# Modulation products of a two-block transformer kernel: column chunks side by side in the free dimension, against four chunks stacked in the partitions

## The reference, cut to what matters

```python
mod = silu(c) @ w_mod_2 + b_mod_2       # (2048) @ (2048, 6 * 2048)
h * (1 + scale) + shift                 # modulate()
```

## Time and profile before

| | |
|---|---|
| median of 3 runs | 2852.14 us |
| the profiled execution: its own time | 2854.0 us |
| its span, first to last instruction | 2852.2 us |
| granted TensorE clock, mean | 0.994 of 2.4 GHz |
| TensorE busy | 2803.9 us, 98% |
| VectorE busy | 2003.3 us, 70% |
| ScalarE busy | 1381.3 us, 48% |
| DMA, mean | 217 GB/s, share of 16 engines in the SP and ScalarE queues 65.7% and 1.5% |

### The profile page before, as it was taken

The page is one execution under the profiler, slowest core; times in us unless marked ns, Lnnn a source line. Parts: engine busy times, 40 slices in busy tenths (PEclk is TensorE's granted clock), DMA queues, the critical chain, the costliest instruction groups (busy, mean ns, idle before and its releaser), DMA issues.

```text
span 2852.2 us, 34653 instructions
## 1 busy us (share of the span) xinstructions
PE 2803.9 (98%) x13089; PEld 2332.8 (82%) x13089; DVE 2003.3 (70%) x2288; ACT 1381.3 (48%) x1730; POOL 150.9 (5%) x108
## 2 busy tenths in 40 slices
PE   9999999999999999999999999999989999999998
PEld 7888888888888888787888888888878888888886
DVE  5666879898798676765785487677975467744455
ACT  5446454443443455546544445754554444344443
POOL 0000010010000100000000001000001000010010
PEclk9999999999999999999999999999999999999999
DMA  7863887888888777655666666308855588765664
GB/s 249 224 193 108 280 280 264 269 277 281 282 273 300 260 244 227 196 191 164 206 195 195 199 186 185 118 9 290 306 177 183 190 277 273 250 184 188 188 190 143
DMA packets 322765, 619.91 MB, mean 217 GB/s; under 512 B 27480, under 2 KB 29176, under 8 KB 321272
## 3 DMA queue, kind: packets, MB, share of 16 engines
q1 hardware_dynamic: 320311, 601.51, 65.7%
q10 hardware_dynamic: 2304, 16.39, 1.5%
HBM read 611.53 MB, written 7.24 MB: 217 GB/s over the span
## 4 chain that ended last, share of the span: by engine, by line
PE 92%; issue 4%; DVE 2%; ACT 1%; DMA 0%; POOL 0%; POOLq 0%; DVEq 0%; ACTq 0%; SPq 0%
PE ps L1371 85%; PE ps L1350 1%; PE ps L1546 1%; PE ps L1756 1%; PE ps L1736 1%; PE ps L1774 1%; PE ps L1504 0%; PE ps L1469 0%; PE ps L1449 0%; DVE res L2116 0%; DVE wlo L1891 0%; PE ps L1599 0%; PE ps L1584 0%; PE ps L1459 0%; DVE macc L2092 0%
## 5 line engine op out<-in xcount | busy, mean ns | idle before, releaser
L1891 DVE TENSOR_TENSOR wlo<-raw,whi 128x1024 fp32r<-128x1024 f32 x940 | 1169.9, 1249 | 735.8 <-ACT whi L697 730.8
L697 ACT ACTIVATE whi<-raw 128x1024 fp32r<-128x1024 f32 x940 | 996.0, 1060 | 1234.4 <-PE ps L1371 1187.7
L1371 PE MATMUL ps<-whi,hhi 128*128 128x512 f32 x2064 | 559.9, 393 | 4.1 <-issue 3.8
L1371 PE MATMUL ps<-whi,hlo 128*128 128x512 f32 x2064 | 553.9, 390 | 0.0
L1371 PE MATMUL ps<-wlo,hhi 128*128 128x512 f32 x2064 | 552.9, 390 | 0.0
L1371 PEld LDWEIGHTS ps<-wlo,hhi 128*128 128x128 f32 x2064 | 388.0, 188 | 81.2
L1371 PEld LDWEIGHTS ps<-whi,hlo 128*128 128x128 f32 x2064 | 387.4, 188 | 81.0
L1371 PEld LDWEIGHTS ps<-whi,hhi 128*128 128x128 f32 x2064 | 384.2, 188 | 83.1 <-issue 6.0
L1371 PE MATMUL ps<-whi,xhi 128*128 128x512 f32 x1632 | 443.6, 394 | 1.6 <-issue 1.6
L1371 PE MATMUL ps<-whi,xlo 128*128 128x512 f32 x1632 | 439.4, 391 | 0.0
L1371 PE MATMUL ps<-wlo,xhi 128*128 128x512 f32 x1632 | 437.3, 390 | 0.0
(11 more groups left out here) (299 smaller groups left out, 1509.1 us busy)
## 6 DMA issues: line engine op xcount, KB each, us to landing
raw<-w_in SPq DMA_DIRECT2D x296, 512.0 KB, 4.3
raw<-mlp_w SPq DMA_DIRECT2D x256, 512.0 KB, 3.8
mraw<-w_mod SPq DMA_DIRECT2D x192, 512.0 KB, 6.3
raw<-w_up SPq DMA_DIRECT2D x128, 512.0 KB, 4.7
raw<-w_down SPq DMA_DIRECT2D x128, 512.0 KB, 5.3
raw<-w_o SPq DMA_DIRECT2D x32, 512.0 KB, 5.8
raw<-w_ple_gate SPq DMA_DIRECT2D x32, 512.0 KB, 4.1
raw<-w_out SPq DMA_DIRECT2D x32, 512.0 KB, 5.0
```

The lines of the kernel that those rows point to most:

```text
L697: nc.scalar.activation(whi[:, s % NSLOT], raw[:, s % NSLOT], ACT.Copy).then_inc(hi_done, 1)
L1371: ins = nc.tensor.matmul(ps[:, bank(par) + th], a[:, kt, th * P:(th + 1) * P], b[:, (s + u) % NSLOT, k], start=(kt == 0 and m == 0), stop= ...
L1891: nc.vector.tensor_tensor(wlo[:, s % NSLOT], raw[:, s % NSLOT], whi[:, s % NSLOT].bitcast(F32), ALU.subtract)\
```

## The change

Tiles are cut another way. A tile takes one part (2048 columns) whole: it has two halves, each 32 rows of `w_mod_2` by 2048 columns, and the four column chunks of 512 lie in four groups of 32 partitions. So 64 row slices instead of 16 row blocks of 128 run through one sum, the accumulator holds a whole part, and after it the partition sum goes over 32 partitions of each group. There are still 192 tiles of 512 KB and the same number of products of 128x512. There are 8 units (six parts, two of them for both vectors) instead of 32: 32 transposes and 8 row sums.

Each half tile has its own DMA, whose source begins with a dimension of 4 chunks and then 32 rows; before, one DMA began with 128 rows. The count of tiles in each chunk is the same. The order of parts is now 2, 0, 1, 3, 4, 5, each for 32 tiles, so the tiles with products for both vectors come in one run of 64. `macc` has two buffers instead of three. The condition vectors are loaded with each run of 32 numbers repeated four times (64 rows each instead of 16). Addresses in `stat` move.

```diff
-    [("b_mod_2", 96), ("c_2", 16), ("c_ctx_2", 16)],
+    [("c_2", 64), ("c_ctx_2", 64)],
...
-    [("hgrn_lb_logits_2", 32)],
+    [("b_mod_2", 96), ("hgrn_lb_logits_2", 32)],
...
+STACK = 4
+ROWS_OF = P // STACK
...
-        macc = at("macc", [P, 2, 3, NCH], F32, lev_at)
+        macc = at("macc", [P, 2, 2, NCH], F32, lev_at)
...
-        MOD_PLAN = [("o", "ss", 0, (0, 4, 6, 6)), ("mlp1", "sbb", 0, (0, 3, 4, 4, 4, 3, 3, 3)), ("mlp1", "bbbs", 8, (4,) * 8),
-                    ("mlp1", "sbbb", 16, (4,) * 8), ("mlp1", "sss", 24, (3,) * 8), ("mix", "ssss", 0, (0, 5, 5, 5, 5, 5, 5, 2)),
-                    ("mlp2", "ssss", 8, (4,) * 8)]
+        MOD_PLAN = [("o", 0, (0, 4, 6, 6)), ("mlp1", 0, (0, 3, 4, 4, 4, 3, 3, 3) + (4,) * 16 + (3,) * 8),
+                    ("mix", 0, (0, 5, 5, 5, 5, 5, 5, 2)), ("mlp2", 8, (4,) * 8)]
+        PARTS = [(2, 1), (0, 2), (1, 2), (3, 1), (4, 1), (5, 1)]
+        PART_LOADS = D // (2 * ROWS_OF)
...
-                        elif name == "c_ctx_2":
-                            src = I[name].rearrange("(b p) -> b p", p=P)
+                        elif name in ("c_2", "c_ctx_2"):
+                            src = bass.AP(I[name].tensor, 0, [[ROWS_OF, rows], [0, STACK], [1, ROWS_OF]])
+                            dst = dst.rearrange("r (a b) -> r a b", a=STACK)
...
-                sp.dma_start(mraw[:, q % MSLOT], w_mod[:, r, :, n * NCH:(n + 1) * NCH]).then_inc(m_landed[q % MSLOT], 16)
+                width = NMOD * D
+                for h in range(2):
+                    src = bass.AP(I["w_mod_2"].tensor, ROWS_OF * (2 * r + h) * width + n * D, [[NCH, STACK], [width, ROWS_OF], [1, NCH]])
+                    sp.dma_start(mraw[:, q % MSLOT, h], src).then_inc(m_landed[q % MSLOT], 16)
...
-                pe.wait_ge(m_mul, MODQ[8 * m + 7][4] + 2 * MODQ[8 * m + 7][3])
+                last = MODQ[PART_LOADS * (m + 1) - 1]
+                pe.wait_ge(m_mul, last[4] + 2 * last[3])
...
-                nc.vector.tensor_reduce(ps[:, MB, n * 8 + v:n * 8 + 8:2], ps[:, 7].rearrange("p (b q) -> p b q", q=P), AX_X, ALU.add)\
+                to = mps[:, n * KT:(n + 1) * KT, v].rearrange("p (j b) -> p b j", j=STACK)
+                nc.vector.tensor_reduce(to, ps[:, 7].rearrange("p (b j q) -> p b j q", j=STACK, q=ROWS_OF), AX_X, ALU.add)\
...
-                dve.wait_ge(m_landed[q % MSLOT], 16 * (q // MSLOT + 1))
-                if r == 0 and m >= 3:
+                dve.wait_ge(m_landed[q % MSLOT], 32 * (q // MSLOT + 1))
+                if r == 0 and m >= 2:
```

More of the change, by code:

```diff
@@ L57 @@
 NCOL = _n
-NCOL_MB = NCOL - 32
+NCOL_MB = NCOL - 128
+LB0 = COL["hgrn_lb_logits_2"]
+STACK = 4
+ROWS_OF = P // STACK
 LEVELS = [64, 32, 16, 8, 4, 2, 1]
@@ L433, in build @@
         w_in, w_o, w_up, w_down = (pieces(I[n][0]) for n in ("w_in", "w_o", "w_up", "w_down"))
-        w_gate, w_ple, w_mod = (pieces(I[n][0]) for n in ("w_ple_gate", "w_ple_proj", "w_mod_2"))
+        w_gate, w_ple = (pieces(I[n][0]) for n in ("w_ple_gate", "w_ple_proj"))
         SEQ = [("U", c) for c in range(4)] + [("D", c) for c in range(4)]
@@ L469, in build @@
         n_pieces = pc[0]
-        N_MCH = NMOD * D // NCH
         MODQ, MOD_AT, SUM_AT, RED_AT = [], {}, {}, {}
         UNITS, UNIT_END = [], []
[L474 to L501, removed]
@@ L502, in build @@
-        assert n_both == 2 * D // NCH and n_one == N_MCH
+        n_ops = 0
+        for name, c0, per in MOD_PLAN:
+            for a in [8 * (c0 + j) + u for j, count in enumerate(per) for u in AT[count]]:
+                m, r = divmod(len(MODQ), PART_LOADS)
+                part, nv = PARTS[m]
+                MOD_AT.setdefault((name, a // 8), {})[a % 8] = len(MODQ)
+                MODQ.append((part, r, m, nv, n_ops))
+                n_ops += 2 * nv
+                if r == PART_LOADS - 1:
+                    for v in range(nv):
+                        at_pe = a + 3 + 2 * v
+                        for table, slot in ((SUM_AT, at_pe), (RED_AT, at_pe + 1)):
+                            table.setdefault((name, slot // 8), {}).setdefault(slot % 8, []).append(len(UNITS))
+                        UNITS.append((m, part, v))
+                    UNIT_END.append(len(UNITS))
+                    if part == 1:
+                        n_ctx_units = len(UNITS)
+            if name == "mlp1":
+                n_mlp1_units, n_mlp1_ops, n_mlp1_mods = len(UNITS), n_ops, len(MODQ)
+            if name == "mix":
+                n_mix_units = len(UNITS)
@@ L567, in vector_loads @@
                     for name, rows in group if gi else ():
+                        dst = vecs[r:r + rows, gi, :]
                         if name == "conv_dw_w_2a":
@@ L925, in _ @@
                                         d_first + 10: context_scale,
-                                        **{d_first + 15 + 2 * g: (lambda g=g: mod_high("normc", g, xhi, mcol[:, 1], modT[:, 0:KT, 1])) for g in range(8)}}))
+                                        **{d_first + 15 + 2 * g: (lambda g=g: mod_high("normc", g, xhi, mcol[:, 1], modT1[:, 0:KT])) for g in range(8)}}))
             def lb_row_out(j):
@@ L2175, in mod_of_mixer @@
                 dve.wait_ge(m_red, n_ctx_units)
-                nc.vector.tensor_tensor(modT[:, 0:NX, 0], mps[:, 0:NX, 0], bmod[:, 0:NX], ALU.add)
-                nc.vector.tensor_tensor(modT[:, 0:NX, 1], mps[:, 0:NX, 1], bmod[:, 0:NX], ALU.add).then_inc(mod_out, 1)
+                nc.vector.tensor_tensor(modT[:, 0:NX], mps[:, 0:NX, 0], bmod[:, 0:NX], ALU.add)
+                nc.vector.tensor_tensor(modT1[:], mps[:, 0:NX, 1], bmod[:, 0:NX], ALU.add).then_inc(mod_out, 1)
             def mod_gain(n, part, c, gain):
-                nc.vector.scalar_tensor_tensor(out=mcol[:, n], in0=modT[:, part * KT:(part + 1) * KT, c], scalar=1.0, in1=col(gain),
+                nc.vector.scalar_tensor_tensor(out=mcol[:, n], in0=(modT1 if c else modT)[:, part * KT:(part + 1) * KT], scalar=1.0, in1=col(gain),
                                                op0=ALU.add, op1=ALU.mult).then_inc(mcol_done, 1)
```

68 lines of the change are left out of this document (36 added, 32 removed).

## The result

The changed kernel takes 3456.77 us (median of four runs, 3441.59 to 3465.26) against 2852.73 us: the ratio is 1.2107, with a 95% interval of 1.2092 to 1.2123, so 604 us slower. The forecast was 3326 us with 3110 to 3620; its direction and cause held, its size was 131 us short.

What follows compares the result with a forecast made beforehand. TensorE was taken to bound the kernel, with DMA next. Packets 524, cushions -60, transposes -10 and clock +20 gave +474 on the profiled 2854.0 us: 3328, forecast as 3326 us, range 3110 to 3620.

Steps and rivals of the forecast that it cites:

- TensorE bounds, DMA is next: In the four stretches with tiles (1087.0 us) TensorE sets the pace; evenly spread DMA has room for 1.1 to 1.2.
- What is removed: On TensorE, 24 units' transposes (8.6 us) and a wait in stage `o` (1.05 us) go: 9.7 us together.
- VectorE's run of tiles: 64 tiles with four products each: VectorE keeps pace, taken as nothing, with 8 us as a bound.
- the second issue: SP issues 192 DMAs more, 90 us of issuing, hidden in its 2185.6 us of waits for VectorE.
- Four engines: Tile sources beginning with 4 go to 4 engines: 18,304 packets at 88 ns take 1,611 us, 524 more than now.
- the four cushions: Work read ahead at the start of each of four stretches hides 15 us each, 60 together (bounds 20 and 72).
- The clock's 20 us: TensorE's clock may fall while it waits in the stretches with tiles: 20 us taken, 100 as the end.
- What does a packet take on a full engine?: A 2048 B packet on a full DMA engine was priced at 88 ns, with ends 81.5 and 93.6 ns.
- Where the stall goes: Late tiles delay pieces in SP's queue; VectorE's product waits for its tile, then TensorE waits for `hi_done` or `lo_done`.
- Rival (c): Four engines carry the tiles, but move a packet in 70 ns: 2976 us; chance 0.04.
- Rival (d): Four engines, and the clock oscillates all the time, some 300 us on top: about 3620 us; chance 0.05.
- the likeliest case's own range: Tiles on four engines at 81.5 to 94 ns a packet: 3171 to 3548 us; chance 0.78.

Runs made afterwards that it cites:

- experiment 1: Changed kernel with partition 4r + j holding row r of chunk j, so each tile's source begins with 32 rows: 2842.36 us against 2853.21, ratio 0.9959.
- 4: Kernel before, with two DMAs of 128 rows for each tile instead of one, all on 16 engines: 2853.86 us against 2853.21, ratio 1.0001.
- 7: Changed kernel with each of VectorE's multiply-adds working on 16 of 512 columns, all waits as before: 3468.56 us in one run.
- experiment 2: Kernel before, with each half tile loaded by a DMA whose source is 4 times 32 rows (permuted rows): 3453.51 us in one run.
- 3: Kernel before, with each half tile loaded by a DMA whose source is 8 times 16 rows: 3034.62 us against 2853.21, ratio 1.0651.
- experiment 5: Changed kernel with the first four matmuls of each piece done twice in chunks with tiles: 3447.33 us in one run.
- experiment 6: Loads alone, no computing, four phases: tiles on 4 engines 499.9 us, on 16 134.0; mixed with pieces, tiles on 4 engines 576.5, on 16 264.2.

## Why the prediction held, point by point

**TensorE bounds, DMA is next.** Right: with DMA even (experiment 1) the stretches take 1075 us with no gaps, with DMA uneven they follow the fullest engine.

**What is removed.** 9.7 us was forecast, 10.9 (7.7 to 15.4) measured in experiment 1, where it can show. In the changed kernel TensorE waits anyway, so the saving can't show.

**VectorE's run of tiles, and the second issue.** Both were taken as nothing. Experiments 1 and 4 bear it out, and 7 shows that even leaving out 259 us of products gains nothing once DMA is the bound.

**Four engines.** Right, by the count of small packets and by experiment 2. The rule of the Trainium skill ("DMA: Bandwidth & Descriptors", "Why a DMA increments its semaphore by 16 and not by 1") is borne out in the number of engines for sources that begin with 4, 8 and 32 (experiments 1 to 3). That all tiles use the same engines fits the times; which engines they are no run shows. The 27 GiB/s that the same page gives for one engine are 29 GB/s, and this isn't borne out: 81 ns for 2048 B are 25 GB/s at best in these runs.

**The size.** The sum was 1087 + 524 - 60 - 10 + 20 = 1561 us for the stretches; they took 1689. The main term of the miss is the packet: taken at 88 ns from windows in which 16 engines shared the work evenly, it is 93.8 ns in the loads alone where four of them also write tiles. 18,304 packets are then 1,717 instead of 1,611 us, 106 more. 1,717 - 1,689 leaves 28 us for the four cushions instead of 60: 32 more. The clock's 20 us weren't seen (experiment 5), nor did the 10 us of transposes show. 106 + 32 - 20 + 10 = 128.

The step that was mis-sized is thus "What does a packet take on a full engine?". Its bounds of 81.5 to 93.6 ns had nearly held it, but no row in the trace of before was the one to go by: that trace has no engine that carries a spread-out transfer and a gathered one at the same time. The split between packets and cushions is worked out and not measured. With the 92.7 ns that a chunk of four tiles shows in the changed kernel itself, the packets are 86 us of the miss and the cushions 52. By 93.8 ns, the stretches in `o`, mixer and `mlp2` come out 9, 14 and 9 us under their packets, and `mlp1` 4 us over them, so it had no cushion at all. That the loads alone price this kernel right and the one of experiment 2 too low by some 90 us says that the price isn't fully understood.

**Where the stall goes.** Right in place for TensorE, which waits for ScalarE, and ScalarE for pieces. Wrong in one link: VectorE's product was to wait for its tile, and VectorE is idle for only 4.5 us in all before its 504 multiply-adds (L2099). And there is one link more: SP itself is held at its issues. Tiles were expected to wait in slots; they wait in SP, and lookahead with them, which is a reason why the cushions may be smaller. That wasn't tested.

**Rival (c), an engine faster than 81 ns,** falls by experiment 6. **Rival (d)** falls by 5: the clock does go up and down (0.82 to 0.89 on average in the stretches), but it costs nothing that was seen. The range was said to reach halfway to (c) and (d); with (d) at about 3620 us its end of 3620 takes all of (d) in. The result lies also in the likeliest case's own range of 3171 to 3548, so this width didn't decide anything.

## What to carry to other kernels

Before changing how a tile is cut, look at the first dimension of the transfer's source: with 4 or 8 there, 4 or 8 engines carried it in these runs, with 32 or 128 all 16 did, and the mean DMA share of the profile doesn't say so. The number of packets under 512 B, less those that the code asks for and divided by the transfers, does. Where a layout needs a small dimension, put it inside and the rows outside (here partition 4r + j instead of 32j + r): so written, the same change is 11 us faster than the kernel before instead of 604 slower.

## What the runs showed of the hardware that I had not expected

A 2 KB packet on a full DMA engine takes 81 to 82 ns when 4 or 8 engines work alone, or when one of two streams goes to HBM, and 86 to 87 ns when 16 engines write evenly into SBUF. When a stream on all 16 engines and one on few both write into SBUF, it takes 93.8 or 88.7 ns with 4 engines, by the pattern of the source, and 104.7 to 106.5 ns with 8. These are single runs of loads alone. The issuing queue is held as well: an issue of a tile's load took 0.47 us in the median before, and 1.7 in the median and 9.3 at most in the changed kernel.
